# Attention of a hybrid diffusion backbone: the value products of two query tiles in one run, ahead of every second tile's scores

## What is computed

```python
def attention(q, k, v):                       # 8 heads, 96 of query/key width, 64 of value width
    ...
    def block(qi):
        s = jnp.einsum('bqhd,bkhd->bhqk', qi, k).astype(jnp.float32) * ATTN_SCALE
        pr = jax.nn.softmax(s, axis=-1).astype(v.dtype)
        return jnp.einsum('bhqk,bkhd->bqhd', pr, v)
    ...
out_c = attention(q, k, v)
mixed = jnp.concatenate([out_a, out_b, out_c], axis=-1)
return jnp.einsum('bnm,md->bnd', mixed, P['w_out'][l]), ckv, k_rope
```

## Time and profile before

| what | us |
|---|---|
| median of 3 runs (lowest, highest) | 1619.80 (1619.73, 1620.74) |
| the profiled execution, its own time | 1615.51 |
| its span from first to last instruction | 1613.7 |
| its PE / DVE / ACT busy time | 1552.2 / 565.1 / 422.4 |
| its mean granted TensorE clock | 0.992 |

### The profile page before, as it was taken

One profiled execution on the slowest core, in us unless ns is written; L12 is line 12 of the kernel. 1 busy time (PEld: TensorE's weight loads), 2 busy tenths in 40 slices (PEclk: granted clock), 3 DMA queues, 4 the chain that ended last, 5 costly groups with the idle time before them and its releaser, 6 DMA issues.

```text
span 1613.7 us, 26717 instructions
## 1 busy us (share of the span) xinstructions
PE 1552.2 (96%) x10773; PEld 1248.0 (77%) x10773; DVE 565.1 (35%) x1373; ACT 422.4 (26%) x964; POOL 105.7 (7%) x108
## 2 busy tenths in 40 slices
PE   4899999999999999999799999999999999999997
PEld 2644545676666666544499999999999999999996
DVE  3101455665656575115766111111111111111114
ACT  4200102554545454224411111111111111111114
POOL 0003500000000000111000100000000000000000
PEclk9899999999999999999899999999999999999999
DMA  8853002001010300431557787787877787877776
GB/s 318 329 217 105 30 0 59 13 1 27 0 26 0 119 6 1 182 117 67 206 197 273 276 278 271 270 303 263 309 256 270 273 308 254 314 252 268 276 234 248
DMA packets 120154, 291.06 MB, mean 180 GB/s; under 512 B 17503, under 2 KB 21126, under 8 KB 116894
## 3 DMA queue, kind: packets, MB, share of 16 engines
q1 hardware_dynamic: 115342, 272.90, 46.5%
q0 software_dynamic: 4752, 17.30, 4.1%
HBM read 266.18 MB, written 21.64 MB: 178 GB/s over the span
## 4 chain that ended last, share of the span: by engine, by line
PE 91%; DVE 4%; DMA 2%; ACT 2%; issue 1%; SPq 1%; DVEq 0%; ACTq 0%
PE ps L1129 30%; PE ps L1158 15%; PE ps L773 9%; PE ps L578 8%; PE ps L874 6%; PE ps L822 5%; PE ps L807 4%; PE ps L639 2%; PE ps L727 1%; PE ps L739 1%; PE ps L752 1%; PE ps L591 1%; DMA x_rows<-wreg 1%; PE ps L1078 1%; PE ps L1086 1%
## 5 line engine op out<-in xcount | busy, mean ns | idle before, releaser
L1129 PE MATMUL ps<-mreg,wreg 128*128 128x144 f32 x4096 | 517.1, 286 | 2.1 <-ACT hreg L1404 2.1
L1129 PEld LDWEIGHTS ps<-mreg,wreg 128*128 128x128 f32 x4096 | 508.8, 190 | 2.5 <-ACT hreg L1404 2.3
L1158 PE MATMUL ps<-mreg,wreg 128*128 128x144 f32 x2048 | 265.6, 286 | 0.5 <-DVE mreg L2047 0.5
L1158 PEld LDWEIGHTS ps<-mreg,wreg 128*128 128x128 f32 x2048 | 257.9, 190 | 0.7 <-DVE mreg L2047 0.7
L2034 DVE TENSOR_TENSOR mreg<-ps,mreg 128x144 f32<-128x144 f32 x120 | 36.9, 308 | 434.1 <-PE ps L1129 434.1
L773 PE MATMUL ps<-wreg 128*128 128x512 f32 (+2 forms) x400 | 171.6, 519 | 0.2
L1432 ACT ACTIVATE mreg<-ps 128x144 f32<-128x144 f32 x128 | 37.1, 290 | 444.7 <-PE ps L1129 444.7
L578 PE MATMUL ps<-hreg,wreg 128*128 128x512 f32 (+1 forms) x432 | 142.9, 489 | 0.0
L874 PE MATMUL ps<-wreg,mreg 128*128 128x512 f32 x288 | 131.8, 601 | 0.0
L807 PEld LDWEIGHTS ps<-const,hreg 128*128 128x128 f32 x648 | 79.8, 141 | 58.8 <-issue 39.3
L578 PEld LDWEIGHTS ps<-hreg,wreg 128*128 128x128 f32 x432 | 70.6, 191 | 69.8 <-issue 69.4
(11 more groups left out here) (270 smaller groups left out, 1131.6 us busy)
## 6 DMA issues: line engine op xcount, KB each, us to landing
wreg<-in_w_e_dram SPq DMA_DIRECT2D x96, 2048.0 KB, 11.7
wreg<-in_w_ada_dram SPq DMA_DIRECT2D x24, 1024.0 KB, 10.0
out_dram<-wreg SPq DMA_DIRECT2D x9, 512.0 KB, 2.6
mreg<-in_x_sample_dram SPq DMA_DIRECT2D x8, 512.0 KB, 7.6
wreg<-in_x_sample_dram SPq DMA_DIRECT2D x8, 512.0 KB, 5.2
wreg<-in_w_out_dram SPq DMA_DIRECT2D x1, 4096.0 KB, 12.7
x_rows<-wreg SPq DMA_DIRECT2D x8, 512.0 KB, 3.3
xn_rows<-wreg SPq DMA_DIRECT2D x8, 512.0 KB, 2.6
```

What stands on the lines that cost most here:

```text
L1129: mm = pe.matmul(o[:, 0:CAP], w[s][:, k, (f % 4) * P:(f % 4 + 1) * P], xsT[b][:, k, :], start=(k == 0), stop=(k == KD - 1))
L1158: mm = pe.matmul(bank[4 + dm % 2][:, 0:CAP], w2[f // 4][:, f % 4, dm * P:(dm + 1) * P], hidT[:, f, :], start=(f == 0), stop=(f == 7))
```

## The change

The products of two query tiles are issued one directly behind the other, in the steps n = 6, 10 and 14; the steps n = 4, 8 and 12 have none. So tiles 1, 3 and 5 keep their place, and tiles 0, 2 and 4 are taken one step later than before. DVE's copies of the results (weighed) follow in the same way, and so does the dealing out of banks 6 and 7. Tiles 6, 7 and 8, behind the loop, stay as they are. The number of instructions is the same on every engine.

```diff
--- before.py
+++ after.py
@@ -826,8 +826,9 @@
 
                 for n in range(2, 16, 2):
                     score(i, n, 0)
-                    if n >= 4:
-                        weigh((n - 4) // 2)
+                    if n in PV_AHEAD_OF:
+                        weigh(n // 2 - 3)
+                        weigh(n // 2 - 2)
                     score(i, n, 1)
                     turn(n - 2, 0)
                     score(i, n, 2)
@@ -1708,7 +1709,11 @@
                     turned(n - 1)
                     highest(i, n + 1)
                     scaled(n)
-                    weighed((n - 2) // 2)
+                    if n + 2 in PV_AHEAD_OF:
+                        weighed(n // 2 - 2)
+                        weighed(n // 2 - 1)
+                    elif n == 14:
+                        weighed(6)
                     scaled(n + 1)
                     if more and n in (4, 6, 8):
                         fold_wq(i + 1, range(n // 2 - 2, n // 2 - 1))
@@ -2252,7 +2257,9 @@
 DVE_TURNS = [(n, 0) for n in range(1, 15, 2)]
 ACT_TURNS = [(n, ch) for n in range(18) for ch in range(3 if n < 16 else 1) if (n, ch) not in DVE_TURNS]
 
-MID_ORDER = [u for n in range(0, 14, 2) for u in [("weigh", (n - 2) // 2)][:n // 2]
+PV_AHEAD_OF = (6, 10, 14)
+
+MID_ORDER = [u for n in range(0, 14, 2) for u in [("weigh", n // 2 - 2), ("weigh", n // 2 - 1)] * (n + 2 in PV_AHEAD_OF)
              + [("turn", m, ch) for m in (n, n + 1) for ch in range(3)]]
 MID_ORDER += [("weigh", 6)] + [("turn", n, ch) for n in (14, 15) for ch in range(3)]
 MID_ORDER += [("turn", 16, 0), ("turn", 17, 0), ("weigh", 7), ("weigh", 8)]
```

## The result

The changed kernel takes 1630.03 us (median of 5 runs, 1628.12 to 1632.02) against 1619.91 us (5 runs of the kernel before, 1619.73 to 1621.35): the ratio is 1.0059, with a 95% interval of 1.0048 to 1.0070. It is 10.1 us slower; +9.8 us and 1629.6 us had been forecast.

What follows compares the result with a forecast made beforehand. PE's own work was taken to bound the kernel. Twelve joins at 1.08 - 0.35 = +0.73 us, 8.8 us, plus 1.0 us once in the last pass, gave +9.8 us: 1629.6 us from 1619.8, range 1625 to 1634.5 us.

Steps and rivals of the forecast that it cites:

- What bounds the kernel: Attention's mid-pass steps: PE's own work alone sets each step, 9.06 us.
- A run of products costs 0.35 us beside its 2.18 us: Edges of a run on PE: 0.35 us lost, saved at each of 12 joins, 4.2 us in all.
- The stall of 1.08 us at `norm_ok`: First transposes in steps n = 4, 8, 12: PE waits for DVE's scaling, 0.93 + 0.05 + 0.10 us.
- The short step: Steps n = 4, 8, 12, without products: 9.06 - 2.18 - 0.35 + 1.08 = 7.61 us.
- Nothing else late: Short steps: exponentials of n end at T + 7.35, before score(n+2,0) at T + 7.61, 0.26 us to spare.
- `routing_tables`: Last pass, step n = 8: PE's stall for the exponentials grows from 0.35 to 1.35 us, +1.0 us once.
- The sum: Whole kernel: 12 joins at +0.73 us, 8.8 us, plus 1.0 us once in the last pass: +9.8 us.
- The switches-only case: Rival at the joins: cheaper shape switches and no stall, 4.2 us saved, 1615.6 us; chance 4%.
- the case of no change: Rival in the short steps: stall and saving cancel at 0.35 us, 1617 to 1623 us; chance 5%.
- the costly join: Rival at the joined runs: a join costs as much as a new run, 4.2 us more, 1633.8 us; chance 7%.
- the clock: Rival in the short steps: stalls lower PE's clock, 1.7 us each, 1650 us if in all 12; chance 2%.
- The thin margin at the exponentials: Rival before score(n+2,0): 0.26 us margin used up, +2.4 to 3.6 us, 1632 to 1633.2 us; chance 12%.

Runs made afterwards that it cites:

- e1: Kernel before plus an unused 512-column row maximum on DVE ahead of every odd unit's maximum; attention grows by 1.6 us.
- e5: Changed kernel with the third score piece ahead of the transposes in short steps; pair of steps 18.67 us, attention 8.4 us longer than in the kernel before.
- e6: e5 plus, in the step before a short one, the last score piece ahead of turn(n-1,1); pair 18.23 us, attention 3.1 us longer than in the kernel before.
- e7: e6 plus, in short steps, highest(n) before scaled(n-1) and turn(n-1,0) later; small DVE work moved to long steps; pair 18.11 us, ratio 0.9993 to the kernel before.

## Why the prediction was right

- **What bounds the kernel**: PE's own work, in equal steps. Held; that is why a shift of DVE's work by 0.6 us was free in e1.
- **A run of products costs 0.35 us beside its 2.18 us.** Held: the joined run took 4.52 us (2 x 2.18 + 0.15), so the join itself is free, as taken, and a change of shape was saved in each of 12 places: 7.65 - 1.10 = 6.55 us is what PE's own work takes in a short step, 9.06 - 2.18 - 0.35 = 6.53 had been expected. The trace agrees with the drain rule of the Trainium skill (TensorEngine Tiling (Array Packing), Key Properties) in that joining saves time on PE; the direction that this rule by itself gives, 4.2 us faster, did not come, because what the products had covered was worth more. That it is a drain which costs the 0.35 us is not shown. A part of it looks like late weights: in the kernel before, the score piece behind a run of products loads its weights only as it starts (398.26), while the score at 394.97 had its load begun 0.11 us ahead, and a late start cost a score 0.10 us elsewhere too.
- **The stall of 1.08 us at `norm_ok`**: 402.78 - 401.73 = 1.05 us, and the four transposes behind it take 0.49 instead of 0.44 us: 1.10 us. Its parts were a little off in opposite directions. From the end of DVE's scaling to PE's start it is 0.13 us in the nine waits of passes 0 to 2 and 0.05 us in the three of the last pass (I had 0.05 us for all, from a wait for ACT in the last pass), and the late weights cost 0.05 us (I had 0.10 us, from a score piece). That the two cancel in nine steps of twelve is luck, of 0.08 and 0.05 us.
- **The short step**: 7.65 us in passes 0 to 2 and 7.58 in the last, for 7.61 us; the long one 11.25 for 11.24. Per join +0.77 us, +0.70 us in the last pass, for +0.73 us.
- **Nothing else late**: held with the exponentials; PE waited for ACT at score(n+2,0) only next to `routing_tables`. The exponentials of unit n end at T + 7.28 (7.35 forecast), 0.37 us ahead of that score, 0.30 us in the last pass (0.26 forecast). In n = 8 of passes 0 to 2 it is only 0.18 us, because `fold_wq` stands ahead of the maximum there; the prediction had not looked at it. e5 and e6 show how near that second wait lies: as soon as PE comes earlier, it sets the step.
- **`routing_tables`**: the short step n = 8 of the last pass takes 8.86 us, 1.28 us more than its neighbours with 7.58, and the score behind it 0.10 us, where I had 1.35 us for both. ACT's sum ends at T + 8.80 (I had T + 8.81) and the score starts at T + 8.86. I had not seen that PE stops twice on the way: by the starts, its last two transposes are 0.66 us late, for DVE's copy behind the maximum (L1705), and the score 0.63 us more, for ACT (the list of waits, which has idle time alone, gives 0.5 and 0.4 us). The first stop costs nothing of its own, since the second ends later.
- **The sum**: +9.8 us forecast, +10.07 us in attention, +10.1 us between the medians.
- **The rivals.** The switches-only case fell with the 12 waits, the case of no change with the 7.64 us step, the costly join with the run of 80 records, the clock with its 1.00 in both windows. The thin margin at the exponentials was not used up in this change, but was in e5 and e6.

The repair was less well foreseen: I expected 18.0 us a pair from e7, and 1.5 to 2 us off attention, and got 18.11 and 0.63 us, because I had counted 0.1 to 0.2 us of waiting for `norm_ok` and not the 0.14 us for the bank behind it.

## What to carry to other kernels

Work that an engine does while it would otherwise wait for a result is cover; before such work is moved or joined with another piece, compare its length with how early the awaited result is there. Here the cover was 2.5 us long, the result 1.6 us early, and the difference of 0.9 us, with up to 0.2 us more for the late start, was paid 12 times for a saving of 0.35 us. Making steps unequal also needs room on the other engines in the short ones: DVE had 5.9 us and ACT 5.2 us of work in a short step, whose own work on PE is 6.5 us, so the saving came out, less than half of it, only after their order had been rebuilt with it.

## What was not expected of the hardware

- A transpose that waits for `norm_ok` starts 0.13 us after the end of DVE's scaling in passes 0 to 2 (402.65 to 402.78) and 0.05 us after it in the last pass (604.12 + 0.89 = 605.01 to 605.06), so the same wait has two prices in one kernel. Passes 0 to 2 are the hardware loop, the last is written out, but the loop alone doesn't make the difference: in it, a score piece starts 0.05 us after ACT's sum (e5), and a transpose that waits for its bank 0.05 us after DVE's copy (e7). Why this one wait costs more in the loop stays open.

```profile
604.12 0.89 DVE L1694 TENSOR_SCALAR hreg<-hreg,stat 128x1280 f32<-128x1280 f32 x1
605.06 0.65 PE L807 MATMUL ps<-const,hreg 128*128 128x128 f32 x4 [0.83 <-DVE hreg L1694]
```

- Outside attention, in code that no kernel here changed, profiled executions differ by up to 7 us (947.6 to 954.9 us behind the last product). The shortest one, e5, and the kernel before with 949.4 us have fewer stretches at the lower clock there. The two windows below begin 138.9 us behind the start of the last product in both kernels: the kernel before is at 1.00, the changed one at 0.94 (e5 is at 1.00 too). So a single total can't tell an effect of 2 us in this kernel; the lengths of the steps can.

```profile
803.22:857.22 54.00, 49.34 (x402) 48.61 (x402) 39.07 (x139) 11.91 (x36) 1.49 (x3) 1.00 0.68 243
```

```profile
816.00:870.00 54.00, 49.34 (x375) 48.74 (x375) 36.51 (x130) 10.33 (x30) 1.49 (x3) 0.94 0.63 230
```

The first window is of the kernel before, the second of the changed one. What makes the clock stay lower there was not tried.
